# An expert trunk on one core: the routing of the tokens cut into three parts, the last tile's final sum moved to TensorE, and the root's table read early

## The reference

```
g_logits = t @ w_group + b_group                  # 4 groups
g_sel = argmax(g_logits)
e_logits = (t @ w_router + b_router)[g_sel]       # 8 experts of that group
top_p, top_i = top_k(softmax(e_logits), 2)        # two experts for each token
top_p = top_p / sum(top_p) * g_prob[g_sel]
...
hid = silu(xb @ w1[e]) * (xb @ w3[e]);  y = hid @ w2[e]
x = x + sum over both experts of top_p * y
return rmsnorm(x, final_norm)
```

## Time and profile before

| | us |
|---|---|
| median of 3 runs | 1359.05 (1358.71 to 1360.3) |
| the profiled execution's own time | 1358.68 |
| its span, first to last instruction | 1356.9 |
| PE busy (share of the span) | 1206.7 (89%) |
| DVE busy | 532.0 (39%) |
| ACT busy | 407.3 (30%) |
| data moved | 295.25 MB |

### The profile page before, as it was taken

One profiled execution on the slowest core, in us unless ns is written; L12 is line 12 of the kernel. 1 busy time (PEld: TensorE's weight loads), 2 busy tenths in 40 slices (PEclk: granted clock), 3 DMA queues, 4 the chain that ended last, 5 costly groups with the idle time before them and its releaser, 6 DMA issues. The chain is left out here.

```text
span 1356.9 us, 15418 instructions
## 1 busy us (share of the span) xinstructions
PE 1206.7 (89%) x6082; PEld 803.1 (59%) x6082; DVE 532.0 (39%) x949; ACT 407.3 (30%) x673; POOL 95.1 (7%) x127
## 2 busy tenths in 40 slices
PE   6999999999999999999999793999977997877781
PEld 5887877686778788888887583333333333333330
DVE  5324454567768348745355644111010010000014
ACT  6234443344543442243243321112111111111112
POOL 2000000000000000000000001211111111111100
PEclk9999999999999999999999995999999999999996
DMA  7222212212022222343413654899999999999995
GB/s 272 95 92 81 96 67 99 94 63 75 34 74 90 93 74 99 107 155 101 164 65 122 278 217 163 300 416 406 410 420 389 411 402 413 419 416 417 413 399 201
DMA packets 49436, 295.25 MB, mean 218 GB/s; under 512 B 8711, under 2 KB 8983, under 8 KB 20053
## 3 DMA queue, kind: packets, MB, share of 16 engines
q1 hardware_dynamic: 40340, 273.48, 51.6%
q0 software_dynamic: 8448, 18.69, 4.1%
q10 hardware_dynamic: 576, 2.10, 0.4%
HBM read 290.21 MB, written 12.93 MB: 223 GB/s over the span
## 5 line engine op out<-in xcount | busy, mean ns | idle before, releaser
L1799 PE MATMUL e_u<-w_raw,xT 128*64 128x512 f32 x1056 | 242.9, 606 | 54.3 <-DMA w_raw<-in_w 51.2
L1799 PEld LDWEIGHTS e_u<-w_raw,xT 128*64 128x64 f32 x1056 | 81.0, 139 | 211.5 <-issue 207.8
L2118 DVE SCALAR_TENSOR_TENSOR tn<-tn,e_u 64x512 f32<-64x512 f32 x33 | 22.4, 680 | 423.8 <-ACT tn L2027 423.8
L291 DVE TENSOR_TENSOR s_lo<-s_raw,s_hi 128x2048 fp32r<-128x2048 f32 (+1 forms) x68 | 138.6, 2038 | 55.4 <-ACT s_hi L286 54.8
L286 ACT CAST s_hi<-s_raw 128x2048 fp32r<-128x2048 f32 (+1 forms) x68 | 115.9, 1704 | 110.2 <-PE pz L594 41.1
L1809 PE MATMUL e_y<-w_raw,hidT 128*64 128x512 f32 x528 | 122.3, 606 | 15.4 <-ACT hidT L2022 15.4
L562 PE MATMUL pz<-hT_hi,s_hi 128*128 128x512 f32 x288 | 116.4, 404 | 0.0
L562 PE MATMUL pz<-hT_hi,s_lo 128*128 128x512 f32 x288 | 113.0, 393 | 0.0
L562 PE MATMUL pz<-hT_lo,s_hi 128*128 128x512 f32 x288 | 113.0, 392 | 0.0
L2017 ACT COPY xT<-e_x 128x512 f32<-128x512 f32 x33 | 19.3, 586 | 311.5 <-PE e_x L1784 311.5
L578 PE MATMUL pz<-hT_hi,s_hi 128*128 128x512 f32 x256 | 102.2, 399 | 0.5
(11 more groups left out here) (368 smaller groups left out, 1869.9 us busy)
## 6 DMA issues: line engine op xcount, KB each, us to landing
w_raw<-in_w SPq DMA_DIRECT2D x192, 1024.0 KB, 27.6
s_raw<-in_w_mix SPq DMA_DIRECT2D x30, 1024.0 KB, 4.9
s_raw<-in_w_gb SPq DMA_DIRECT2D x32, 768.0 KB, 4.3
s_raw<-in_w_out_pieces SPq DMA_DIRECT2D x4, 1024.0 KB, 4.8
w_raw<-ys_scratch SPq DMA_DIRECT2D x8, 512.0 KB, 7.0
x_sb<-in_x SPq DMA_DIRECT2D x4, 512.0 KB, 4.9
rel_bias<-in_rel_tiles POOLq DMA_DIRECT2D x8, 256.0 KB, 3.0
decay<-in_decay POOLq DMA_DIRECT2D x8, 256.0 KB, 4.2
```

Of the source, the lines that this page charges most:

```text
L291: nc.vector.tensor_tensor(w_lo[n % 2][:, 0:w], w_raw[n % 2][:, 0:w], w_hi[n % 2][:, 0:w].bitcast(F32), ALU.subtract).then_inc(w_split, 1)
L1799: m = nc.tensor.matmul(ps_u[o][lo:lo + FIRST, :], xT[b][:, k * FIRST:(k + 1) * FIRST], raw[j][:, kk * FF:(kk + 1) * FF], start=k == 0, sto ...
L2118: nc.vector.scalar_tensor_tensor(tn[:], tn[:], 1.0, ps_u[b][0:FIRST, :], ALU.add, ALU.mult).then_inc(s_hm, 1)
```

## The change

**The choice in three parts.** What DVE did for four tiles at once is done for tile 0 (right behind the normed tile 2), for tiles 1 and 2 together, and for tile 3 (`ROUTED`). Counting and places come in two parts, tiles 0 to 2 and tile 3 (`PLACED`). PE makes the logits of tile 0 behind group 4 and no longer behind group 5. The last tile's second half is copied out of PSUM by ACT, not by DVE. `idx` alone releases POOL; `idy`, the counts and the weights `wsel` are made behind it. The counting result is read from PSUM without a copy `pos`. The ones `ones_b` are written by DVE at the start of the second block (before: by POOL in the first). POOL's two writes of zeros to `xs` wait for the last group of matmuls (`e_mm`, 8) and no longer for the attention's values (`e_o`, 4), because `xs` has changed places with the choice's work area.

**The last tile's final sum by PE.** DVE makes two diagonal matrices of the tile's weights (`weight_diag`), and PE adds x and both weighted results in PSUM: two matmuls with the identity, four with the diagonals. ACT and DVE read that sum from PSUM. DVE's order at the end becomes sums 0, sums 1, scale 0, sums 2, scale 1, 2, 3.

**The root's table early.** A root of one column stands at ACT's start and another behind its last expert.

```diff
@@ POOL, first block
-                nc.gpsimd.memset(ones_b[:], 1.0).then_inc(r_fl, 1)
-                pool.wait_ge(e_o, MX_HEADS)
+                pool.wait_ge(e_mm, 2 * T)
                 for b in range(2):
                     nc.gpsimd.memset(xs[b][:], 0.0).then_inc(r_fl, 1)
...
-                pool.wait_ge(r_idx, 1)
                 pool.reg_mov(last_x, N - 1)
                 for b in range(2):
                     pool.wait_ge(s_xw[b], 16 * T // 2)
+                pool.wait_ge(r_idx, 1)
@@ PE, first block
+                    if g == 4:
+                        logits(0)
                     if g == 5:
                         rows_turned_3(1)
-                        logits(0)
...
+                for b, (lo, hi) in enumerate(PLACED):
+                    pe.wait_ge(r_hot, b + 2)
+                    for t in range(lo, hi):
+                        o = pa[3 * b][:, t * EXPERTS:(t + 1) * EXPERTS]
+                        for q in range(t):
+                            nc.tensor.matmul(o, before_ones[:, P:2 * P], hot2[:, q, :], start=(q == 0), stop=False)
+                        last = nc.tensor.matmul(o, before_ones[:, 0:P], hot2[:, t, :], start=(t == 0), stop=True)
+                    last.then_inc(r_pc, 1)
@@ ACT, first block
+                act.wait_ge(c_ones, 4)
+                nc.scalar.activation(root_of[:], gn_eps[:], ACT.Sqrt)
...
+                act.wait_ge(r_tb, T)
+                nc.scalar.copy(h3T[(T - 1) % 2][:, 4:8, :], pa[5][:].rearrange("p (k n) -> p k n", k=4)).then_inc(r_ea, 1)
@@ DVE, first block
+                    if t == T - 2:
+                        routed(0)
+                routed(1)
+                routed(2)
+                for b in range(len(PLACED)):
+                    placed(b)
+                dve.wait_ge(r_it, 1)
...
+                nc.vector.tensor_tensor(idx[:], idf[:], second[:], ALU.add).then_inc(r_idx, 1)
@@ DVE, second block
+                do.after(nc.vector.memset(ones_b[:], 1.0))
@@ PE, end
+                pe.wait_ge(s_hd, TURNS)
+                for half in range(2):
+                    nc.tensor.matmul(ps_u[half], ident[:], x_sb[:, T - 1, half * FF:(half + 1) * FF],
+                                     start=True, stop=False)
+                pe.wait_ge(f_diag, 2)
+                for ch in range(2):
+                    pe.wait_ge(f_ld[ch][T - 1], 16)
+                    for half in range(2):
+                        last = nc.tensor.matmul(ps_u[half], weight_diag[:, ch, :],
+                                                y_of(T - 1, ch)[:, half * FF:(half + 1) * FF],
+                                                start=False, stop=ch == 1)
+                last.then_inc(f_last, 1)
@@ ACT, end
+                nc.scalar.activation(early[:], ident[:, 0:1], ACT.Sqrt)
@@ DVE, end
+                sums(0)
+                sums(1)
+                scale(0)
+                sums(2)
+                for t in range(1, T):
+                    scale(t)
```

More of the change, by code:

```diff
@@ L338, in trunk @@
             nmax_m, rsum_m = (sbuf(c, "m_" + n, [P, MX_HEADS * T]) for n in ("nmax", "rsum"))
-            job_area = Area(-(-nc.sbuf_base // 32) * 32, scratch.end - 8 * KB_ - (-(-nc.sbuf_base // 32) * 32))
-            act_b, rank, ones_b = (job_area(n, [P, JOB_BLOCKS]) for n in ("act_b", "rank", "ones_b"))
+            after_stats = -(-nc.sbuf_base // 32) * 32
+            choice = Area(after_stats, scratch.end - 8 * KB_ - after_stats)
+            sel = choice("sel", [P, T, PER_GROUP])
+            top_r = choice("r_top", [P, 2, T, PER_GROUP])
+            topi = choice("topi", [P, 2, T, PER_GROUP], U32)
+            topf = choice("topf", [P, 2, T, PER_GROUP])
+            oh = choice("oh", [P, T, GROUPS])
+            sm = choice("r_small", [P, 8, T])
+            e_of, dest = choice("e_of", [P, 2, T]), choice("dest", [P, 2, T])
+            hot2 = choice("hot2", [P, T, EXPERTS], F32R)
+            second = choice("second", [P, EXPERTS])
             pz = [psum(c, f"pz{j}") for j in range(2)]
@@ L408, in finished @@
                     eng.wait_ge(z_mm, 2 * (MIX_PIECES + n - MEM0) + 2)
+            ROUTED, PLACED = ((0, 1), (1, T - 1), (T - 1, T)), ((0, T - 1), (T - 1, T))
+            SLOT_ORDER = [(ch, t) for lo, hi in PLACED for ch in range(2) for t in range(lo, hi)]
             def place_free(eng, place):
@@ new lines, in placed @@
+                def placed(b):
+                    lo, hi = PLACED[b]
+                    s = slice(lo, hi)
+                    at = pa[3 * b][:, lo * EXPERTS:hi * EXPERTS].rearrange("p (t e) -> p t e", t=hi - lo)
+                    dve.wait_ge(r_pc, b + 1)
+                    for ch in range(2):
+                        do.after(nc.vector.tensor_tensor(junk_r[:, ch, s, :], hot[:, ch, s, :], at, ALU.mult))
+                        do.after(nc.vector.tensor_reduce(dest[:, ch, s], junk_r[:, ch, s, :], AX_X, ALU.add))
+                    for ch in range(2):
+                        for t in range(lo, hi):
+                            nc.vector.tensor_scalar(at_slot[:, ch * T + t, :], slot_no, dest[:, ch, t:t + 1], None,
+                                                    ALU.is_equal).then_inc(r_at, 1)
@@ L1703, in trunk @@
         with ExitStack() as c:
-            act_area, out_area = Area(beyond + 8 * KB_, 16 * KB_), Area(top - 8 * KB_, 8 * KB_)
+            act_area, out_area = Area(beyond, 16 * KB_), Area(top - 8 * KB_, 8 * KB_)
+            job_area = Area(after_stats, top - 8 * KB_ - after_stats)
+            act_b, rank, ones_b = (job_area(n, [P, JOB_BLOCKS]) for n in ("act_b", "rank", "ones_b"))
             few = Area(after_tables, table_area.end - after_tables)
@@ L1718, in trunk @@
             jobs, jobsi = few("jobs", [P, 4]), few("jobsi", [P, 4], I32)
+            early = few("early", [P, 1])
+            weight_diag = Area(after_stats, top - 8 * KB_ - after_stats)("weight_diag", [P, 2, P])
             ps_x, ps_h = psum(c, "e_x", (P, KD * FIRST)), psum(c, "e_h", (P, KF * FIRST))
-            ps_u, ps_y = ([psum(c, f"e_{n}{b}") for b in range(2)] for n in "uy")
+            ps_last = psum(c, "e_u", (P, D))
+            ps_u = [ps_last[:, b * FF:(b + 1) * FF] for b in range(2)]
+            ps_y = [psum(c, f"e_y{b}") for b in range(2)]
             ys_halves = ys_dram.rearrange("s (h d) -> (s h) d", h=2)
@@ L1745, in trunk @@
             f_ld = [[sem(f"f_ld{ch}{t}") for t in range(T)] for ch in range(2)]
-            f_x, f_ss, f_ms, f_sq, f_o, f_done, f_gain = (
-                sem("f_" + n) for n in ("x", "ss", "ms", "sq", "o", "done", "gain"))
+            f_x, f_ss, f_ms, f_sq, f_o, f_done, f_gain, f_diag, f_last = (
+                sem("f_" + n) for n in ("x", "ss", "ms", "sq", "o", "done", "gain", "diag", "last"))
             END = [p for p in ORDER if AT[p] >= AT[ORDER[-1]] + 1 - DEPTH][:T + 1]
@@ L2148, in _, with sums @@
                 experts(JOB + 1, TURNS)
-                def scale(t):
-                    dve.wait_ge(f_sq, t + 1)
-                    do.after(nc.vector.reciprocal(ss[:, t:t + 1], ss[:, t:t + 1]))
-                    if t == 0:
-                        dve.wait_ge(f_gain, 16)
-                    nc.vector.scalar_tensor_tensor(x_sb[:, t, :], x_sb[:, t, :], ss[:, t:t + 1], final_gain,
-                                                   ALU.mult, ALU.mult).then_inc(f_o, 1)
-                for t in range(T):
+                for ch in range(2):
+                    nc.vector.tensor_scalar(weight_diag[:, ch, :], ident[:], wsel[:, ch, T - 1:T], None, ALU.mult
+                                            ).then_inc(f_diag, 1)
+                def sums(t):
                     for ch in range(2):
@@ L2165, in _, with scale @@
                     ins.then_inc(f_x, 1)
-                    if t:
-                        scale(t - 1)
+                def scale(t):
                     dve.wait_ge(f_ss, t + 1)
```

180 lines of the change are left out of this document (85 added, 95 removed).

## The result

The changed kernel took 1350.82 us (median of 10 runs, 1348.21 to 1353.2) where the kernel before took 1358.82 (10 runs, 1353.2 to 1360.3) beside it: a ratio of 0.9947, 95% interval 0.9936 to 0.9959. Between the medians that is 8.0 us less, by the ratio 7.2, and the time lies outside the range of 1352.9 to 1357.0. One of the 36 runs of the kernel before beside a0 took 1425.01 us, at a mean granted clock of 0.834 where the others had 0.970 or more, and is left out of the ratios. For the size they agree only where they overlap, 0.9950 to 0.9959, some 5.6 to 6.8 us, where I had forecast 4.5.

The account below looks back on a forecast made before the run. Weight loading, DMAs busy at 409 GB/s, was taken as the bound from 860 to 1320 us. Gains 0.8 + 3.4 - 0.2 + 0.5 = 4.5 took 1358.68 to 1354.2; adding 0.4 gave 1354.6, range 1352.9 to 1357.0.

Parts of the forecast that it names:

- the hole: Gap in DMA traffic before the weight stream, nothing at 834 to 838 us; should shrink as `idx` comes earlier.
- PE is at half clock by then: In the choice, at the logits of tile 2: they cost 3.60 us at half clock, against 1.87 at full.
- 3.4 late: In the choice: tile 3's logits, the last, end at 823.5 instead of 820.12 us.
- The choice, 3.4 forecast: Choice of experts before the weight stream: `idx` ready at 832.7 instead of 836.11, a gain of 3.4 us.
- The start, 0.8: Kernel start: moving the 1.28 us table load under the wait for x gains 0.8 us, between nothing and 1.28.
- The second block, -0.2: Start of the second block: writing `ones_b` on DVE ahead of the jobs' table costs 0.2 us, between nothing and 0.3.
- The end, 0.5: Kernel end: PE making tile 3's final sum gains 0.5 us, between a gain of 2.1 and a loss of 0.5.
- The stream, one for one: Weight loading: each microsecond that `idx` comes earlier starts the stream, and ends the kernel, a microsecond earlier.
- Theory B: From the experiments, not the prediction: the weight stream also runs faster once it starts earlier, by some 2 us.
- POOL did not hold DVE: First rival, 25%: in the choice, POOL's zeros for `xs` hold DVE, tile 3's chain 0.9 to 1.8 us later; 1355.5 to 1356.4.
- the second rival: 17%: PE stays at half clock when the second block starts, first places free 2.3 to 4.6 us later; 1356.8 to 1359.
- More: 6%: full clock at the end or in the logits of tile 2, giving 1352.5 to 1353.5 us.

Follow-up runs that it names:

- a0: The changed kernel itself, unchanged, measured a second time beside the kernel before: 1351.72 us against 1356.96, ratio 0.9961.
- e1: The changed kernel with the choice in parts alone, the last-tile sum by PE and the early root's table taken back: 1354.17 us, ratio 0.9974 against before.
- e9: The changed kernel with the first operation on the finished table of rows done 24 times over as a delay: 1355.89 us, ratio 0.9988 against before.
- e5: The changed kernel with the first part of the choice (tile 0) moved behind the loop over the tiles: 1349.5 us, ratio 0.9946 against before.
- e6: The changed kernel with the table of ones written in the first block, in a place of its own: 1351.12 us, ratio 0.9961 against before.
- e7: The changed kernel with PE kept busy up to the last landing by multiplications nobody reads: 1351.65 us, ratio 0.9958 against before.
- e3: The kernel before with only the early read of the root's table at the start added: 1357.12 us, ratio 1.0005 against before.
- e4: The changed kernel with PE kept busy in the gaps of the choice by multiplications nobody reads: 1349.38 us, ratio 0.9945 against before.

## Why the prediction was wrong

The direction, the place and the mechanism were right: the hole shrinks with the table of rows, and the end comes earlier by as much. What failed is the step "PE is at half clock by then", with which I priced the logits of tile 2 at 3.6 us and made the last logits "3.4 late". That is true in three of the seven profiles of kernels with the choice in parts and no clock held in it (a0, e1, e9) and false in four (the changed kernel's, e5, e6, e7), where they took 1.97 or 1.98. The row that I gave for it, 0.50 in the earlier trace rows, begins at 822. In the execution that I read the clock fell at 813.2, and my chain had these logits begin at 813.4: the step rested on 0.2 us, and the moment of the fall moves by more than that from execution to execution, from 811.6 to 815.5 in the choices in parts. I took it for a property of the program. The logits of tile 2, which the change puts on the chain at just this time, now meet the fall or don't, and that is 1.65 us.

The step is not all of the miss. The two profiled executions lie 9.0 us apart where I had 4.5. Of the 4.5 us between, the choice has 2.6 (1.65 the clock, 1.0 the rest of the chain), the stream 2.4, which is scatter as told below, the end 0.3; the start took back 0.2 and the second block 0.8 (0.2 more lie outside the spans).

- **The choice, 3.4 forecast.** 28.5 to 24.1 is 4.4 us where both kernels have the lower clock, and 28.5 to 22.5 is 6.0 where the changed one still has the higher. Over the profiles without a clock held in the choice it is 27.9 (four of before's choice) against 23.1 (changed, a0, e1, e6, e7), so 4.8. 1.0 us of this is there even at half clock: the last logits of a0 end at 823.76, 14.4 us behind the turned tile 2, where my chain had 14.9, and from there the gather follows in 9.8 where I had 10.2. The parts themselves were well sized: 3.7 for 3.8, tile 3's second sum 1.7 late for 1.9, `routed(1)` 5.0 for 5.1.
- **The start, 0.8.** PE's first matmul of the mix moved from 18.44 to 17.45, more than said. By the turned tile 2 it is lost in the scatter: 808.9 on the mean of five profiles without the early table, 808.3 of nine with it (808.6 without e5's, the earliest). e3 alone shows no gain, 1.0005. The Trainium skill (ScalarE: Activation LUTs, What ACT_TABLE_LOAD costs) would have had up to 2.7 us here. The load moved to 0.94 took 1.28 and its read followed it at 2.24 with nothing between, and the 0.99 gained is less than the 1.28 alone.
- **The second block, -0.2.** It was -0.7 on the mean (16.2 in seven profiles with the write against 15.5 in the five whose choice is that of before) and -1.0 between the two profiles. The write itself cost 0.27. What I left out is that it moves the rest of DVE's chain against POOL's issues, where two operations then lose 0.2 each. That made 0.75 at the jobs' table (14.24 to 14.99), of which 0.25 reached the ring between e6 and the changed kernel.
- **The end, 0.5.** -0.3 to 1.2 as made, 0.5 on the mean (11.4 in five profiles with DVE's sums, 10.9 in seven with PE's). Right, and PE's sums took 5.13 to 6.73 us by the clock, between the 3.67 and 7.0 that I had.
- **The stream, one for one.** Held. The 2.4 us by which it looked faster in the changed kernel's profile (493.0 to 490.6) are scatter: five profiles whose choice is that of before have 490.0 to 493.0 (mean 492.0), nine others 489.5 to 493.4 (mean 491.5). Theory B is out with it.
- **The rivals.** POOL did not hold DVE: its zeros began at 808.20 and the cast before them at 807.85. PE's first block of 32 took 9.69 us, under the 10 of the second rival, and the 32 behind it 7.09 at full clock, where I had 6.9. "More", at 6%, had its condition come true, full clock in the logits of tile 2; but its range, 1352.5 to 1353.5, was too slow as well, so it was no better priced than the forecast.

The terms measured over the profiles are 0.6 + 4.8 - 0.7 + 0.5 = 5.2 us. That is the second measurement (5.2), and under the interval of the first (5.6 to 8.7). What the first has beyond it is partly that its ten runs of before lay high: 1358.8, where 36, 26 and 17 runs beside the experiments had medians of 1357.0, 1356.4 and 1357.4. Why they differ was not found. The range was too narrow for a second reason, then: it stood on one execution's 1358.68 and a median of three runs, while single runs of one kernel lie 5 to 8 us apart.

## What to carry to other kernels

Before a term is taken from a row at half clock, find the window in which the clock falls, and see how far the row is from it. If the two are close, the row has two prices, and both belong in the range, for the changed kernel as for the one before. Where a change moves short matmuls of TensorE into a gap, ask what is left of the clock there, and try a few multiplications that nobody reads: in the choice they brought some 2 us here. Take the base of the forecast from many runs, not from one. To judge a change of 5 us under a scatter of 7, measure the distance between two landmarks of the trace around it, in several profiles, and not the time of the whole.

## What the hardware showed that I had not expected

- The same program on the same data has its TensorE at full clock at one place in one execution and at half clock in the next: 1.98 and 3.63 us for the same 16 matmuls, 5.61 and 6.57 for the last eight. The Trainium skill (TensorE: Matmul & The Clock Gate, What's actually happening) says that the ramp up to full clock differs from run to run of one kernel, and advises not to fit to it as it is under 1% of a kernel. Here it is the fall that differs, by up to 7.8 us, and what hangs on it is small as well: 1.65 us are 0.12% of this kernel, but over a third of what the change was forecast to give.
- Two multiplications of 512 columns in a gap of 1.9 us, and a short one in the next gap, kept the clock up: in e4 it was 1.00 from 812 to 818, with the logits of tile 2 at 814.23. In the three kernels with such multiplications in the choice it fell at 823.0 or later, in the eleven others at 819.4 or earlier, ten of them by 815.5.
- A DVE operation over 257 columns took 0.52 instead of 0.29 us, and one over 32 columns 0.44 instead of 0.24, when it began 0.57 us behind the start of the issue of one of POOL's indirect transfers and not 0.18 or 0.05 behind it. Removing a write of 0.27 us ahead of them shortened the chain by 0.75.
